# The attention branch's output product moves from the blend into the recurrence

## The reference, cut to what matters

```python
h = rms_norm(x, norm1_g) * (1.0 + scale1) + shift1
p = h @ w_in
q, k, v, f_logit, p_rwkv, gate_logit = jnp.split(p, IN_SPLITS, axis=-1)
o_fox = fox_attention(q, k, v, log_f)                      # 1024 x 512
o_rwkv = rwkv7_branch(token_shift(p_rwkv, shift_mu), ...)  # 1024 x 512, recurrent over tokens
g_fox, g_rwkv = jnp.split(jax.nn.sigmoid(gate_logit), 2, axis=-1)
merged = g_fox * (o_fox @ w_out_fox) + g_rwkv * (o_rwkv @ w_out_rwkv)   # two 512 x 1024 products
x = x + gate1 * (merged @ w_o)
h2 = rms_norm(x, norm2_g) * (1.0 + scale2) + shift2
x = x + gate2 * hier_moe(h2, ...)      # 32 experts, top 2
return rms_norm(x, final_g)
```

## Time and profile before

| | us |
|---|---|
| median of 3 runs | 1740.7 (1730.34 to 1747.76) |
| the profiled execution | 1735.84 |
| its span in the profile | 1734.1 |
| busy in the span: TensorE, VectorE, ScalarE, GpSimd | 1603.0, 851.0, 488.0, 355.2 |

### The profile page before, as it was taken

One profiled execution on the slowest core, in us unless ns is written; L12 is line 12 of the kernel. 1 busy time (PEld: TensorE's weight loads), 2 busy tenths in 40 slices (PEclk: granted clock), 3 DMA queues, 4 the chain that ended last, 5 costly groups with the idle time before them and its releaser, 6 DMA issues. The chain is left out here.

```text
span 1734.1 us, 33929 instructions
## 1 busy us (share of the span) xinstructions
PE 1603.0 (92%) x14226; PEld 1166.4 (67%) x14226; DVE 851.0 (49%) x1351; ACT 488.0 (28%) x921; POOL 355.2 (20%) x703
## 2 busy tenths in 40 slices
PE   5999999999989996898989999979999999899996
PEld 5688887878877883677877878845555555454542
DVE  4655456797546765677856455671111111111114
ACT  1642111133326773554542132231000000000002
POOL 1100011120002003466742011111222222121211
PEclk9999999999998996888989999989999999999998
DMA  9357766524248711313164433486999999999987
GB/s 330 144 184 277 255 207 225 190 70 135 84 146 217 174 52 56 72 44 80 25 204 153 151 100 111 176 351 263 372 423 424 422 423 422 424 421 420 386 331 301
DMA packets 144713, 400.67 MB, mean 231 GB/s; under 512 B 49108, under 2 KB 65543, under 8 KB 127025
## 3 DMA queue, kind: packets, MB, share of 16 engines
q1 hardware_dynamic: 114306, 330.88, 51.7%
q0 software_dynamic: 15504, 41.34, 6.5%
q10 hardware_dynamic: 14752, 26.29, 4.1%
HBM read 344.89 MB, written 64.18 MB: 236 GB/s over the span
## 5 line engine op out<-in xcount | busy, mean ns | idle before, releaser
L3274 PE MATMUL psum<-w,ex_x_t 128*64 128x256 f32 x1376 | 156.9, 384 | 7.5 <-DMA w<-in_exp_w 6.6
L3274 PEld LDWEIGHTS psum<-w,ex_x_t 128*64 128x64 f32 x1376 | 97.6, 138 | 60.6 <-DMA w<-in_exp_w 10.0
L3434 DVE TENSOR_TENSOR ex_sig_m<-psum,ex_sig_m 128x256 f32<-128x256 f32 x32 | 13.6, 425 | 241.1 <-ACT ex_sig_m L3398 241.1
L3398 ACT ACTIVATE ex_sig_m<-psum 128x256 f32<-128x256 f32 x32 | 12.3, 384 | 388.0 <-PE psum L3274 388.0
L192 PE MATMUL psum<-w_even,h_hi 128*128 128x512 f32 (+1 forms) x320 | 117.7, 368 | 0.0
L193 PE MATMUL psum<-w_even,h_lo 128*128 128x512 f32 (+1 forms) x320 | 117.7, 368 | 0.0
L191 PE MATMUL psum<-w_even,h_hi 128*128 128x512 f32 (+1 forms) x320 | 117.7, 368 | 0.0
L3319 PE MATMUL psum<-w,ex_hid_t 128*64 128x512 f32 x336 | 81.8, 631 | 7.1 <-issue 6.6
L3179 POOL TENSOR_TENSOR ex_spare<-neghalf 128x1 f32<-128x1 f32 x79 | 14.9, 189 | 348.2 <-DVE ex_y L3444 344.1
L3444 DVE TENSOR_TENSOR ex_y<-psum,mod_bc 128x512 f32<-128x512 f32 x32 | 22.1, 692 | 125.4 <-PE psum L3319 125.4
L3274 PE MATMUL psum<-w_mixed,ex_x_t 128*64 128x256 f32 x640 | 71.9, 381 | 1.8 <-DMA w_mixed<-in_exp_w 1.2
(11 more groups left out here) (575 smaller groups left out, 3913.2 us busy)
## 6 DMA issues: line engine op xcount, KB each, us to landing
w<-in_exp_w SPq DMA_DIRECT2D x64, 2048.0 KB, 37.0
w_mixed<-in_exp_w SPq DMA_DIRECT2D x31, 2048.0 KB, 29.4
w_ring<-in_ada_w SPq DMA_DIRECT2D x12, 2048.0 KB, 10.8
w_ring<-in_w_in SPq DMA_DIRECT2D x6, 2048.0 KB, 11.7
w_ring<-in_w_in SPq DMA_DIRECT2D x9, 1024.0 KB, 5.6
qk<-stage_r ACTq DMA_DIRECT2D x16, 512.0 KB, 7.5
bl_gates<-gates SPq DMA_DIRECT2D x8, 1024.0 KB, 4.8
w<-pair_rows SPq DMA_DIRECT2D x16, 512.0 KB, 10.8
```

The lines of the kernel that those rows point to most:

```text
L3274: last = mm(ps[h * MAIN:(h + 1) * MAIN, j * FH:(j + 1) * FH], x_t[:, k, 0:MAIN], w[:, k, h * FH:(h + 1) * FH], start=(k == 0), stop=(k == ...
L3434: nc.vector.tensor_tensor(sigm[:], ps[:, 0:n], sigm[:], ALU.mult).then_inc(sig(f"silu_{kind}"), 1)
```

## The change

The attention branch's product becomes 16 items: item n is the product of token tile n mod 8 with column half n // 8, 12 matmuls to a PSUM bank that the recurrence leaves free at that point. Each is placed in TensorE's hand-written order inside the recurrence: items 0, 1, 2 in round -2, 3 to 6 in round -1, 7 in round 0 ahead of `gates(1)`, 8 to 12 in rounds 2 to 6 ahead of `gates(3)` to `gates(7)`, 13 and 14 in place of the four unread matmuls, 15 ahead of the last `w_rows`. ScalarE reads each result to SBUF, issues its store (256 KB) to a new tensor `fox` in memory, and issues the load of item n+2's operand (512 KB). `attend` now stores `o_fox_t` as a high and a low part (128 KB an item) which ScalarE and VectorE make where VectorE alone copied. Of `w_out_fox` one column half at a time is loaded and split, the first in `attend`, the second in rounds 1 and 2; it lies where `mod_bc[:, 0:4]` lies, so the load of `mods` goes to the end of the blend. The blend keeps 24 matmuls a tile, splits only `o_rwkv`, has two PSUM banks for each half, and loads `fox` (512 KB a tile) instead of `o_fox_t`.

```diff
@@ attend
-        o_t = sb("att_o", [P, OUT, P])
+        o_t = sb("att_o", [P, OUT, 2, P], F32R)
...
-            sp.dma_start(keep["mod_bc"][:, 0:4, :].rearrange("p a n -> p (a n)"),
-                         dram["mods"].partition_broadcast(P).rearrange("p a n -> p (a n)")).then_inc(sig("mods_in"), 16)
+            sp.dma_start(keep["sum_1"][:, 1], fox_rows(ins, 0)).then_inc(sig("raw_in0"), 16)
...
+            def read_high(n):
+                act.wait_ge(sig("mixed"), n + 1)
+                if n >= OUT:
+                    act.wait_ge(sig(f"o_out{n % OUT}"), 16 * (n // OUT))
+                nc.scalar.activation(o_t[:, n % OUT, 0, :], bank[6 + n % 2][:, 0:P], ACT.Copy).then_inc(sig("o_hi"), 1)
...
-                nc.vector.tensor_copy(o_t[:, n % OUT, :], bank[6 + n % 2][:, 0:P]).then_inc(sig("o_read"), 1)
+                dve.wait_ge(sig("o_hi"), n + 1)
+                nc.vector.tensor_tensor(o_t[:, n % OUT, 1, :], bank[6 + n % 2][:, 0:P], o_t[:, n % OUT, 0, :].bitcast(F32), ALU.subtract).then_inc(sig("o_read"), 1)
...
+FOX_AT = {0: 4, 1: 7, **{t: t + 5 for t in range(3, TT)}}
+FOX_READ = [8, 8] + list(range(9, 14)) + [15]
@@ recur, SyncE
+                if t < 2:
+
+                    sp.wait_ge(sig("y_full"), 2 * (TT - 1 + t))
+                sp.wait_ge(sig(f"fox_out{t % 2}"), 16 * ((TT + t) // 2 + 1))
+                sp.dma_start(fox_in[:, t % 2, :], dram["fox"][t * P:(t + 1) * P, :]).then_inc(sig(f"fox_tile_in{t % 2}"), 16)
...
+                if t == 1:
+
+                    sp.wait_ge(sig("fox_full"), TT)
+                    sp.dma_start(fox_raw, fox_rows(ins, 1)).then_inc(sig("raw_in1"), 16)
...
+            sp.wait_ge(sig("fox_full"), ITEMS)
+            sp.dma_start(keep["mod_bc"][:, 0:4, :].rearrange("p a n -> p (a n)"),
+                         dram["mods"].partition_broadcast(P).rearrange("p a n -> p (a n)")).then_inc(sig("mods_in"), 16)
             for c in range(KT // 2):
                 sp.wait_ge(sig(f"raw_in{c}"), 32)
+            sp.wait_ge(sig("mods_in"), 16)
@@ recur, ScalarE
+            def load_item(n):
+                tok = slice(n % TT * P, (n % TT + 1) * P)
+                act.dma_start(fox_o[:, n % 2].bitcast(F32).rearrange("p a k n -> p (a k) n"),
+                              dram["o_fox_t"].rearrange("a (k p) n -> p (a k) n", p=P)[:, :, tok]).then_inc(sig(f"fox_in{n % 2}"), 16)
+
+            def fox_out(n):
+
+                act.wait_ge(sig("fox_full"), n + 1)
+                if n >= 2:
+                    act.wait_ge(sig(f"fox_out{n % 2}"), 16 * (n // 2))
+                copy(fox_y[:, n % 2, :], fox_bank(n), "fox_read")
+                act.wait_ge(sig("fox_read"), n + 1)
...
+                act.dma_start(dram["fox"][rows_t, cols], fox_y[:, n % 2, :]).then_inc(sig(f"fox_out{n % 2}"), 16)
+                if n + 2 < ITEMS:
+                    load_item(n + 2)
...
                 at(t - 2, read_w, read_sa(0))
+                if t in FOX_AT:
+                    fox_out(FOX_AT[t])
                 at(t, gates, keys_v)
...
+                if t == 2:
+                    act.wait_ge(sig("raw_in1"), 16)
+                    copy(fox_w[:, 0], fox_raw, "fox_w_hi")
...
-            weights_high(0, 2)
-            at(last, expand(0), expand(1))
+            fox_out(13)
+            weights_high(0, 1)
+            at(last, expand(0))
+            fox_out(14)
+            at(last, expand(1))
@@ recur, TensorE
                     if i == FIRST_LEVEL:
+                        pe.wait_ge(sig("fox_read"), FOX_READ[t])
...
+            def fox(n):
...
+                half, b = n // TT, n % 2
+                if n >= 2:
+                    pe.wait_ge(sig("fox_read"), n - 1)
+                if half:
+                    pe.wait_ge(sig("fox_w_lo"), 1)
...
+                matmul3(nc, fox_bank(n), [((fox_o[:, b, 0, k, :], fox_o[:, b, 1, k, :]), (fox_w[:, 0, k, :], fox_w[:, 1, k, :]))
+                                          for k in range(WK)]).then_inc(sig("fox_full"), 1)
...
-            for _ in range(4):
-                mm(bank[3], const["ones"][:], const["gate_row"], start=True, stop=True)
+            fox(13)
+            fox(14)
@@ recur, VectorE
                 at(t + 1, masked(1))
+                if t == 2:
+                    dve.wait_ge(sig("fox_w_hi"), 1)
+                    tt(fox_w[:, 1], fox_raw, fox_w[:, 0].bitcast(F32), ALU.subtract).then_inc(sig("fox_w_lo"), 1)
                 at(t, bonus_values)
...
-                    tt(m, bank[4 + 2 * half], g[:, cols], ALU.mult).then_inc(sig("fox_gated"), 1)
+                    tt(m, fox_in[:, t % 2, cols], g[:, cols], ALU.mult).then_inc(sig("fox_gated"), 1)
```

More of the change, by code:

```diff
@@ L1225, in _ @@
             nc.scalar.activation(ident_r[:], const["ident"][:], ACT.Copy).then_inc(sig("mask_r"), 1)
-            for n in range(N + 2):
+            for n in range(N + 4):
+                at(n - 4, read_high)
+                if n == TT:
+                    act.wait_ge(sig("raw_in0"), 16)
+                    nc.scalar.activation(keep["s1"][:, 0], keep["sum_1"][:, 1], ACT.Copy).then_inc(sig("fox_w_hi"), 1)
                 at(n - 2, evacuate(0, 0))
@@ L1300, in recur_buffers, with over @@
     }
+def over(place, nc, name, shape, dt):
+    with nc.sbuf_tensor(name, shape, dt) as tensor:
+        return tensor
 def blend_buffers(nc):
@@ L1310, in blend_buffers @@
              "gates": sb("bl_gates", [P, 2, 2 * D]), "o_in": sb("bl_o_in", [P, 2, 2, W]),
+             "fox_in": over(place, nc, "bl_fox_in", [P, 2, 2, D], F32)[:, :, 0, :],
              "o_r": sb("bl_o_r", [P, 2, 2, 2, W], F32R), "mixed": sb("bl_mixed", [P, 2, D]),
@@ L1447, in recur, with fox_bank @@
         WK = W // P
+        fox_in, fox_o, fox_y = late["fox_in"], keep["fox_o"], keep["fox_y"]
+        fox_w, fox_raw = keep["s1"], keep["sum_1"][:, 1]
+        ITEMS = 2 * TT
+        def fox_bank(n):
+            return bank[n % 2] if n < ITEMS - 1 else bank[5]
         block = ctx.enter_context(nc.Block("recur"))
@@ L1848, in high @@
                     act.wait_ge(sig("branches_full"), 2 * (t - 1))
-                act.wait_ge(sig(f"o_fox_in{b}"), 16 * (t // 2 + 1))
-                copy(o_r[:, b, 0, 0, :], o_in[:, b, 0, :], "o_fox_hi")
                 act.wait_ge(sig("o_flipped"), t + 1)
                 copy(o_r[:, b, 1, 0, :], bank[b], "o_rwkv_hi")
+            for n in range(2):
+                load_item(n)
             for t in range(-2, TT):
@@ L2153, in _ @@
                 at(t - 1, doubled(5, 1))
+                if t == -1:
+                    fox(3)
                 at(t + 1, products(0))
@@ L2157, in _ @@
                 at(t - 1, own_keys, past_keys(0))
+                if t + 1 in FOX_AT:
+                    fox(FOX_AT[t + 1])
                 at(t + 1, gates, keys_v)
@@ L2161, in _ @@
                 at(t + 2, logits)
+                if t < 0:
+                    fox(5 * (t + 2))
                 at(t + 1, turn_r)
@@ L2168, in _ @@
                 at(t + 2, sum_before)
+                if t == -2:
+                    fox(1)
                 at(t, doubled(4, 0))
                 at(t + 2, chunk_sums)
+                if t < 0:
+                    fox(2 + 4 * (t + 2))
                 at(t, doubled(4, 1))
@@ L2403, in _ @@
                 gate_both(s)
-def load_rows(sp, sig, raw, first, src):
-    src = src.rearrange("(k p) n -> p k n", p=P)
-    for k in range(0, src.shape[1], 2):
-        sp.dma_start(raw[:, first + k:first + k + 2, :], src[:, k:k + 2, :]).then_inc(sig(f"raw_in{(first + k) // 2}"), 16)
 def weight(w, e):
```

104 lines of the change are left out of this document (57 added, 47 removed).

## The result

| | us |
|---|---|
| before | 1730.3 median of 10 executions (1725.8 to 1747.8) |
| changed | 1748.7 median of 10 executions (1740.4 to 1757.3) |
| ratio | 1.0085, 95% interval 1.005 to 1.012 |
| profiled execution, before and changed | 1735.8 and 1747.4; spans 1734.1 and 1745.6 |
| forecast | 1727.7, range 1706 to 1752 |

The change was to bring 13 us and costs 15 (by the ratio) to 18 (by the medians). In the spans of the two profiled executions it is +11.5: the outward stage starts 13.2 us later than before, and from there on the two traces differ by 1.7. So the loss lies ahead of `outward`. By stage, from the starts of the functions on TensorE in both traces (changed minus before): start to the first `flip_lora` +3.6, recurrence **+47.2** (264.9 to 312.1), `flip_o(0)` to `outward` **-37.6** (107.3 to 69.7).

A forecast was written before the change was run, and what follows sets the result against it. TensorE bounds the blend; in the recurrence it partly waits, partly runs at 1.2 GHz, and GpSimd's chain sets later rounds. -39.5 + 10 + 1 + 4 - 1.5 + 4.2 + 6.8 + 2 = -13.0: 1740.7 to 1727.7 us, range 1706 to 1752.

The forecast's parts named there:

- The blend: Blend stage: 24 matmuls a tile leave, a steady tile falls from 12.5 to 6.9 us; -39.5 us in all.
- The +4 for transfers: Blend tiles 2 to 5: 11 MB of loads take 33 us against 27.4 of TensorE, lateness not made up; +4 us.
- The failed step: Recurrence, rounds 1 and 3 to 6: small allowance for the items' transfers beside the inversion's; +1, -1.5 and +4.2 us.
- 4.0 of landing: Round 3, item 9: `compact` lands in 4.0 us, so the stretch to `offset` falls no lower than 8.3 us.
- a fair share is 1 us of delay a round: Rounds 4 to 6: each item's store and load delays the inversion chain's transfers by 1 us a round.
- -1.5 + 4.2: Item 9 in round 3 fills a wait, -1.5 us; items 10 to 12 in rounds 4 to 6 cost +4.2 us.
- the slower rival: Rounds -1 to 6: items' transfers hold up the inversion chain, up to 6 us a round, +42, 1767 us; chance 0.12.
- +1: Round 1: SyncE waits for item 7 ahead of `inverse_in`, and a copy enters ScalarE ahead of the flips; +1 us.
- Start and filling rounds: Recurrence start, items 0 to 7: added matmuls partly fill idle TensorE time, plus two load issues; +10 us, range +3 to +18.
- Item 8: Round 2: it waits for the split weights, comes behind the gram wait and delays `gates`; +4 us, range 0 to +8.
- Last tile: Recurrence tail: items 13 to 15 and ScalarE's copies and issues delay `offset`, `doubled` and `w_rows`; +6.8 us, range +3 to +9.
- Attention: Attention stage: ScalarE gets 32 copies, one weight split, a copy and double-size store at the end; +2 us, range 0 to +7.

The follow-up runs named there:

- second trace: The changed kernel run once more with nothing edited: 1755.7 us, ratio 1.0122 to the kernel before.
- late: Changed kernel with stores and next loads of items 7 to 12 issued behind `expand(1)`, second weight half loaded a round later: 1721.0 us, ratio 0.9927.
- best version: late, plus items 13 and 14 shipped behind the last tile's `expand(0)` and `expand(1)`, `w_o` 1 MB a tile over four tiles: 1714.8 us, ratio 0.9889.

## Why the prediction was wrong

**The blend** was right to 2 us. Forecast 105 to 65 us from the first product, -39.5; measured 104.5 to 67.2, **-37.3**. A steady tile takes 6.9 us as forecast. (Its +4 was not worked out: 33 us of transfers against 27.4 of TensorE are 5.6, and -43.7 and 4 are -39.7.) The +4 for transfers is seen where it was put, TensorE in front of `flip_o(4)` and `flip_o(5)` behind the two halves of `w_o`:

```profile
997.70 0.66 PE L2206 MATMUL psum<-ident,bl_o_in 128*128 128x128 f32 x4 [2.85 <-DMA bl_o_in<-o_rwkv]
...
1007.26 0.66 PE L2206 MATMUL psum<-ident,bl_o_in 128*128 128x128 f32 x4 [0.90 <-DMA bl_o_in<-o_rwkv]
```

and spreading `w_o` gave 4.7 us back, in a kernel that also moves issues in the tail. `mods` was issued at 1022.7 and landed at 1033.3, ahead of the end of the stage.

**The failed step** is the price of the items' transfers for `compact`, in the terms of rounds 3 to 6 and of round 1: "4.0 of landing", as before, beside item 9, and "a fair share is 1 us of delay a round" beside items 10 to 12. From `gates(3)` to `gates(7)` the sum had -1.5 + 4.2 = +2.7. Measured are +10.7 (126.8 for 116.1 us) and +5.9 in the second trace; with the issues moved -7.3 (late) and -7.7 (best version). Four things were wrong in it:

- The size beside item 9. "Not below the arrival of `compact`" gave 8.3 us from `gates(4)` to `offset` of tile 3, with a landing of 4.0. The landing took 7.9 us and the stretch 10.8 (808.63 to 819.44). With the issues moved the landing took 3.7 and the stretch 7.2:

```profile
798.84 1.02 PE L2083 MATMUL psum<-gate_w,lora_t 128*128 128x512 f32 x2
...
806.05 0.19 PE L2100 MATMUL psum<-inv,gram 64*64 64x32 f32 x1
```

- The share of the traffic as a measure. Round 4 as a whole has a DMA share of 0.30 for 0.26 before, and while the list was under way it was 0.89, against 0.87 in the late version: neither tells a landing of 7.9 us from one of 3.7. (The three numbers 1.5, 1 and 1.7 are not worked out from the 1 us a round and the 2.8 of item 12 either.)
- The reason against it. The sentence and the slower rival name `inverse_in` beside `blocks_out` and `blocks_in`, but what spoke against the rival, "the load starts later than `blocks_out`", holds for `blocks_out` alone. It does start later, by 1.7 us (808.09 and 809.83). But it starts 0.3 us *ahead of* `inverse_in`, and behind that stand ScalarE, which works in order, and TensorE's `offset`.
- The same step is missing in round 1. There "+1" counted a wait of SyncE and a copy; the 1 MB load that SyncE issues 0.4 us ahead of `compact` wasn't counted as a transfer at all. Measured +4.5; with both late -2.5 in the late version and +0.6 in the best.

Of the 22.7 us that the recurrence took over its forecast, rounds 1 and 3 to 6 hold 11.5 (3.5 and 8.0), the filling rounds 3.9, item 8 2.5, the tail 2.4 and what stands behind it 2.4. That the step carries more than its own rounds is shown by the late version: with every matmul and transfer in place and only the issues moved, the recurrence is +18.7 over before where the sum had +24.5, and the whole time is 1721.0 us.

This is the third rival, which had a chance of 0.12 and a price of +42 for seven rounds of 6 us. The mechanism was its own; its size lay between: moving the issues gives 28.5 us back in the recurrence and 27.7 in the whole time. The rule of the Trainium skill that the prediction cited beside it ("DMA: Bandwidth & Descriptors", Issuing engines are not separate DMA queues: transfers of ScalarE and SyncE share the 16 engines and interleave) agrees with the traces: ScalarE's load of 6.7 us and SyncE's `compact` of 7.9 ran beside each other, and `compact` took 3.7 where the load left later.

That 1748.7 us lies inside the range of 1706 to 1752 is luck: the range stands on a median of three executions before the change (1740.7), and ten gave 1730.3. Counted from that, the forecast would be 1717 and the range 1696 to 1742.

**The other terms.** Start and filling rounds: +10 forecast (3 to 18), measured +13.9 from the first `flip_lora`, and 1.7 us more between the attention and it; 10.1 go with the matmuls, so the nature was right and the size a little low. Item 8: +4 forecast, +6.5 measured, and +5.7 to +7.9 in the other traces that have its 12 matmuls and split the weights where the change does; `gates(3)` stood late behind an item that came after the masked gram, as said. Last tile: +6.8 forecast, +9.2 measured to `w_rows`, of which 3 went with the late issues of the rounds ahead and 5.8 more with ScalarE's issues moved behind `expand`: +0.3 is left. (No run parts the time that ScalarE takes to issue them from what their transfers hold up.) The part of the sum that read "ScalarE's copy and two issues 1.8" in front of `expand` was right in place, and avoidable. Behind `w_rows` +2.4, not in the sum. Attention: +2 forecast; from its first score to its last product 127.1 us before and 128.7 in the profiled execution of the change; 128.3 to 132.7 in all kernels with it, +1 to +6.

What I had set down as signs came: `keys_v` at 1.15 us, in all eight rounds (before, it was near 2 us in most), the last `offset` 8.4 us behind `y_squares` (938.91 to 947.31). And so did the sign of the slower case, GpSimd waiting for `rw_blocks_u` over 6.25 us in most rounds: in seven of eight, longest 14.2 (the view of waits above). It is a weaker sign than I took it for, since before it was over 6.25 in four of eight already.

## What to carry to other kernels

When work is moved into a loop that waits on a small transfer, list every DMA that the move issues, and for each small transfer on the loop's path ask what is issued in the microsecond ahead of it or just behind it, on any engine. The mean traffic of a round says nothing of it: the DMA share in round 4 rose only from 0.26 to 0.30. The small load landed 1 to 3 us later with 512 KB issued 1.4 us ahead, and 4 us later with a 256 KB store and the 512 KB load 0.7 and 0.3 us ahead. Issued behind the wait that the small one ends, store and load left its landing at 3.0 to 4.9 us (2.9 to 5.2 before the change), and moving these issues and the weight half turned a ratio of 1.0085 into 0.9927.

## What the runs showed that I had not expected

- 128 KB of block list landed 7.9 us after its issue beside 768 KB issued 0.3 and 0.7 us ahead from another engine; 9.1 with 1 MB issued 0.4 us ahead and the 768 KB 0.2 and 0.6 us behind; 5.9 and 6.0 with the 1 MB alone; and 3.0 to 4.9 in all eight rounds of the late version.
- With the items' matmuls in TensorE's waits the steady rounds are *faster* than before once nothing is late. From `gates(3)` to `gates(7)` the best version takes 108.4 us at clock 1.00 (row above), the kernel before 116.1 at 0.87, with VectorE busy 88.8 and 88.7 us. The clock is what differs in the rows; that it is all of the gain was not tested:

```profile
753.00:869.10 116.10, 107.75 (x2448) 90.94 (x2448) 88.67 (x149) 58.44 (x144) 78.35 (x136) 0.87 0.24 54
```

- Transfers that only the end of the blend and `outward` need (`w_o`, 4 MB) cost it 4.7 us by their grouping, 2 MB in each of two tiles against 1 MB in each of four.
- A run whose experiment alters the data that decides routing can't be judged by its whole time: the two that did so took 89 and 90 us more from the router's last product to the end, with nothing changed there. That it is the routing wasn't looked at.
